# Block 2 of a two-block model on one core: recurrence without GpSimd, output product begun tile by tile, narrower waits at three stage borders

## The reference, cut to what matters

```python
q, k, v, u, y_branch, g_att, g_rec = jnp.split(z, SPLITS, axis=-1)
y_att = neighbourhood_attention(q, k, v, rpb[l]) @ w_att_o[l]
u = centred_depthwise_conv(u, conv_w[l], conv_b[l])
h_fwd = rg_lru(u, w_rg_a[l, 0], b_rg_a[l, 0], w_rg_i[l, 0], b_rg_i[l, 0], lru_lambda[l, 0], False)
h_bwd = rg_lru(u, w_rg_a[l, 1], b_rg_a[l, 1], w_rg_i[l, 1], b_rg_i[l, 1], lru_lambda[l, 1], True)
y_rec = ((h_fwd + h_bwd) * jax.nn.gelu(y_branch)) @ w_rec_o[l]
mixed = jax.nn.sigmoid(g_att) * y_att + jax.nn.sigmoid(g_rec) * y_rec
x = x + mixed @ w_out[l]
...
def rg_lru(u, w_a, b_a, w_i, b_i, lam, reverse):
    r_gate = jax.nn.sigmoid(block_diag_linear(u, w_a, b_a)).astype(jnp.float32)
    i_gate = jax.nn.sigmoid(block_diag_linear(u, w_i, b_i))
    log_a = -LRU_C * r_gate * jax.nn.softplus(-lam.astype(jnp.float32))
    a = jnp.exp(log_a)
    mult = jnp.sqrt(jnp.maximum(-jnp.expm1(2.0 * log_a), 0.0))
    bx = mult * (i_gate * u).astype(jnp.float32)
```

## Time and profile before

| | us |
|---|---|
| median of 3 runs | 2997.16 (2996.86 to 3001.26) |
| the profiled execution | 2997.03 |
| its span, first to last instruction | 2995.2 |
| TensorE busy in it | 2883.7 (96%) |
| VectorE, ScalarE, GpSimd busy | 1736.0, 1310.8, 279.7 |
| mean granted TensorE clock | 0.984 |

### The profile page before, as it was taken

The page is one execution under the profiler, slowest core; times in us unless marked ns, Lnnn a source line. Parts: engine busy times, 40 slices in busy tenths (PEclk is TensorE's granted clock), DMA queues, the critical chain, the costliest instruction groups (busy, mean ns, idle before and its releaser), DMA issues.

```text
span 2995.2 us, 34460 instructions
## 1 busy us (share of the span) xinstructions
PE 2883.7 (96%) x13080; PEld 2283.8 (76%) x13080; DVE 1736.0 (58%) x2404; ACT 1310.8 (44%) x2112; POOL 279.7 (9%) x167
## 2 busy tenths in 40 slices
PE   7999999999999999998999999998999999999997
PEld 5777777888888878886766777776787888878885
DVE  4333355235866666777455425998324866666785
ACT  4444452114655544454354314666114555554452
POOL 4122410000000000001222101222000000000000
PEclk9999999999999999999999999999999999999998
DMA  3111111113344385440312111111113343375441
GB/s 113 36 36 37 42 36 43 57 57 126 127 155 150 135 305 165 152 133 22 135 50 58 35 57 45 54 43 43 49 42 120 130 155 144 152 281 179 152 137 57
DMA packets 84971, 302.70 MB, mean 101 GB/s; under 512 B 9424, under 2 KB 9552, under 8 KB 78544
## 3 DMA queue, kind: packets, MB, share of 16 engines
q1 hardware_dynamic: 83088, 294.31, 28.7%
q10 hardware_dynamic: 1728, 6.29, 0.7%
HBM read 225.07 MB, written 75.50 MB: 100 GB/s over the span
## 4 chain that ended last, share of the span: by engine, by line
PE 56%; issue 33%; DVE 6%; ACT 3%; POOL 2%; DMA 0%; POOLq 0%; DVEq 0%; SPq 0%; ACTq 0%
PE ps L2230 16%; PE ps L371 12%; PE ps L2496 5%; PE pa L2496 5%; PE ps L2525 4%; PE pa L2525 4%; PE ps L2374 2%; PE pa L2274 2%; PE pa L2302 1%; PE ps L2541 1%; PE pa L2283 1%; DVE th L2063 1%; POOL tm L699 1%; POOL sqsum L617 1%; DVE tm L2066 1%
## 5 line engine op out<-in xcount | busy, mean ns | idle before, releaser
L361 DVE TENSOR_TENSOR w_lo<-w_raw,w_hi 128x1024 fp32r<-128x1024 f32 x134 | 181.4, 1355 | 516.8 <-ACT w_hi L355 516.7
L355 ACT ACTIVATE w_hi<-w_raw 128x1024 fp32r<-128x1024 f32 x134 | 141.3, 1055 | 450.1 <-PE ps L371 292.5
L371 PE MATMUL ps<-a_hi,w_hi 128*128 128x512 f32 x896 | 286.4, 401 | 20.8 <-DVE w_lo L361 9.4
L371 PE MATMUL ps<-a_lo,w_hi 128*128 128x512 f32 x896 | 284.2, 399 | 0.0
L371 PE MATMUL ps<-a_hi,w_lo 128*128 128x512 f32 x896 | 283.5, 398 | 0.0
L2230 PE MATMUL ps<-a_hi,w_hi 128*128 128x512 f32 x704 | 237.3, 418 | 22.7 <-DVE w_lo L361 10.1
L2230 PE MATMUL ps<-a_lo,w_hi 128*128 128x512 f32 x704 | 225.8, 402 | 0.0
L2230 PE MATMUL ps<-a_hi,w_lo 128*128 128x512 f32 x704 | 225.6, 401 | 0.0
L1149 ACT ACTIVATE krh<-k_rraw 128x512 fp32r<-128x512 f32 x192 | 121.1, 630 | 234.2 <-PE ps L2525 124.6
L371 PEld LDWEIGHTS ps<-a_hi,w_hi 128*128 128x128 f32 x896 | 170.6, 192 | 66.0 <-issue 14.8
L1845 DVE TENSOR_TENSOR krl<-k_rraw,krh 128x512 fp32r<-128x512 f32 x192 | 132.7, 691 | 136.0 <-ACT krh L1149 135.5
(11 more groups left out here) (325 smaller groups left out, 6056.3 us busy)
## 6 DMA issues: line engine op xcount, KB each, us to landing
w_raw<-wstream SPq DMA_DIRECT2D x134, 512.0 KB, 3.5
k_rraw<-hff SPq DMA_DIRECT2D x224, 256.0 KB, 2.7
hff<-hbuf SPq DMA_DIRECT2D x32, 1024.0 KB, 3.9
wA<-wff SPq DMA_DIRECT2D x16, 2048.0 KB, 7.8
hff<-hbuf SPq DMA_DIRECT2D x32, 768.0 KB, 3.3
w_raw<-wff SPq DMA_DIRECT2D x32, 512.0 KB, 4.1
f_raw<-wff SPq DMA_DIRECT2D x32, 512.0 KB, 4.5
hres<-zt SPq DMA_DIRECT2D x16, 512.0 KB, 2.6
```

The lines of the kernel that those rows point to most:

```text
L355: nc.scalar.activation(w_hi[:, slot], w_raw[:, slot], ACT.Copy).then_inc(s_whi, 1)
L361: nc.vector.tensor_tensor(w_lo[:, slot], w_raw[:, slot], w_hi[:, slot].bitcast(F32), ALU.subtract).then_inc(s_wlo, 1)
L371: mm = nc.tensor.matmul(out[0:m, c], w[0:kp, slot, wofs:wofs + m], x[0:kp, k, c * HC:(c + 1) * HC], start=first and n == 0, stop=last and ...
```

## The change

1. **GpSimd** does nothing more in `rec`. Its three operations per tile become VectorE instructions: `u_lo`, the sum of the directions at the head of `output`, and `gelu_arg`, one scalar_tensor_tensor that takes the place of both VectorE's polynomial and GpSimd's product.
2. **Guard on ScalarE**: a Relu with scale -1 (L1304 of the changed kernel) between tanh and exp of each direction; VectorE's two guard instructions go. ScalarE's gelu tanh moves behind the square roots, and the one-column tanh `warm` goes.
3. **Release by direction**: the first two gates of a tile wait for the forward scan of the tile before alone, the last two for the backward one. `(1 + i) * u` (`input_part`) is done for both directions as soon as their gates are out.
4. **Order** in a tile on VectorE: input parts, weight split, `gelu_arg`, convolution of the next tile, forward direction, weight split, `u_lo`, `gelu`, backward direction, weight split, output. On ScalarE `u_out` splits the next y unit before it reads u out. The gate unit's split covers the 512 columns that are used, not 1024.
5. **mrg2**: VectorE splits the first weight unit before any `rec_lo`; `rec_hi` of tiles other than 7 waits for scans; TensorE's first projected product waits for its `r_lo` tiles one by one.
6. **out2**: `a_hi`/`a_lo` of tiles 0 to 5 are split before the last two projected products, tiles 6 and 7 right behind their merges; the split of the unit out2+1 comes last on VectorE.
7. **Borders**: VectorE's last `a2_lo` comes before the last weight split of the attention; TensorE enters `gat0`, `rec` and `out2` with waits for the one buffer that each product overwrites, not with `enter`.

```diff
-            nc.scalar.activation(w_hi[:, slot], w_raw[:, slot], ACT.Copy).then_inc(s_whi, 1)
+            nc.scalar.activation(w_hi[:, slot, 0:n], w_raw[:, slot, 0:n], ACT.Copy).then_inc(s_whi, 1)
...
-            u_lo(0)
-            for c in range(KT):
-                pool.wait_ge(sem("s_gpoly"), c + 1)
-                nc.gpsimd.tensor_tensor(gt[:], gt[:], y_in[:, c % 2], ALU.mult).then_inc(sem("s_gin"), 1)
-                if c < KT - 1:
-                    u_lo(c + 1)
-                pool.wait_ge(sem("s_scan"), 2 * c + 2)
-                nc.gpsimd.tensor_tensor(tm[:, 0], tm[:, 0], tm[:, 1], ALU.add).then_inc(sem("s_dirs"), 1)
...
+                if c:
+                    split_hi(act, u + 2, u % 2, (u + 2) // 2, t + 1)
                 nc.scalar.activation(ur[c % 2][:, 2:2 + S], pair_flat(t), ACT.Identity, bias=V("b_in", 12 + c)
...
-                    if c and o == 0:
-                        act.wait_ge(sem("s_scan"), 2 * c)
+                    if c and o % 2 == 0:
+                        act.wait_ge(sem("s_scan"), 2 * c - 1 + o // 2)
...
+                    nc.scalar.activation(tm[:, d], tm[:, d], ACT.Relu, scale=-1.0).then_inc(sem("s_neg"), 1)
...
-                act.wait_ge(sem("s_gin"), c + 1)
-                nc.scalar.activation(gt[:], gt[:], ACT.Tanh, scale=0.7978845608028654).then_inc(s_thr, 1)
                 for d in range(2):
                     act.wait_ge(sem("s_neg"), 2 * c + d + 1)
                     nc.scalar.activation(tm[:, d], tm[:, d], ACT.Sqrt).then_inc(sem("s_root"), 1)
-
-                if c:
-                    act.wait_ge(sem("s_warm"), c)
-                nc.scalar.activation(warm[:], ones[:, 0:1], ACT.Tanh).then_inc(sem("s_warm"), 1)
+                act.wait_ge(sem("s_gin"), c + 1)
+                nc.scalar.activation(gt[:], gt[:], ACT.Tanh, scale=0.7978845608028654 * 0.044715).then_inc(s_thr, 1)
...
+            act.wait_ge(s_mm, st.t + 11)
+            for k in range(6):
+                merged_hi(2, k)
+            split_hi(act, st.u + 15, (st.u + 13) % 2, (st.u + 15) // 2, st.t + 14)
+            merged_hi(2, 6)
+            split_hi(act, st.u + 16, (st.u + 14) % 2, (st.u + 16) // 2, st.t + 15)
+            merged_hi(2, 7)
...
+                    a2_lo(npair - 1)
                     weights(3 * npair + EXTRA)
-                    a2_lo(npair - 1)
...
             for c in range(KT):
-                guards(c)
+                input_part(c, 0)
+                input_part(c, 1)
+                unit_gates(c)
+                gelu_arg(c)
+                if c < KT - 1:
+                    conv(c + 1)
                 direction(c, 0)
                 if c < KT - 1:
                     unit_y(c + 1)
+                    u_lo(c + 1)
+                gelu(c)
                 direction(c, 1)
-                gelu(c)
...
-                st = enter("out2") if b == 2 else STAGES["out1"]
+                st = STAGES[f"out{b}"]
+                if b == 2:
+                    pe.wait_ge(s_outA, st.a)
...
-            st = enter("gat0")
+            st = STAGES["gat0"]
...
-            st = enter("rec")
+            st = STAGES["rec"]
...
+                if t == st.t:
+                    pe.wait_ge(s_outA, st.a)
+                elif t == st.t + 1:
+                    pe.wait_ge(s_outD, st.d)
+                else:
```

More of the change, by code:

```diff
@@ L983, in _, with merged_hi @@
                     unit_split(U_GP + 2 * n + 3)
+            def merged_hi(b, k):
+                if b == 1:
+                    act.wait_ge(sem("s_mrg"), k + 1)
+                else:
+                    act.wait_ge(s_outD, STAGES["mrg2"].d + k + 1)
+                nc.scalar.activation(a_hi[:, k], (mres if b == 1 else res)[:, k], ACT.Copy, scale=0.5
+                                     ).then_inc(sem("s_mhi"), 1)
             def out_stage(b):
@@ L988, in out_stage @@
                 n = 1 if b == 1 else 3
[L989 to L996, removed]
+                if b == 1:
+                    act.wait_ge(s_mm, st.t - 1)
+                    for k in range(KT):
+                        merged_hi(1, k)
                 gain = "g_mlp" if b == 1 else "g_ln2"
@@ L2057, in conv, with input_part @@
                 ins.then_inc(sem("s_conv"), 1)
+            def input_part(c, d):
+                dve.wait_ge(s_outA, st.a + 3 + 6 * c + 2 * d + 2)
+                i = th[:, 2 * d + 1]
+                nc.vector.scalar_tensor_tensor(out=i, in0=i, scalar=1.0, in1=uc[:, c % 2], op0=ALU.add, op1=ALU.mult
+                                               ).then_inc(sem("s_iu"), 1)
             def direction(c, d):
@@ L2074, in direction, with gelu_arg, u_lo @@
                 ins.then_inc(sem("s_scan"), 1)
-            def guards(c):
+            def gelu_arg(c):
                 dve.wait_ge(sem("s_gsq"), c + 1)
[L2080 to L2083, removed]
+                nc.vector.scalar_tensor_tensor(out=gt[:], in0=gt[:], scalar=1.0 / 0.044715, in1=y_in[:, c % 2],
+                                               op0=ALU.add, op1=ALU.mult).then_inc(sem("s_gin"), 1)
+            def u_lo(c):
+                dve.wait_ge(sem("s_uh"), c + 1)
+                if c:
+                    dve.wait_ge(s_mm, st.t + 6 * c + 1)
+                nc.vector.tensor_tensor(ul[:], uc[:, c % 2], uh[:].bitcast(F32), ALU.subtract).then_inc(sem("s_ul"), 1)
             def gelu(c):
@@ L2144, in gated @@
                 nc.vector.tensor_tensor(r, r, zt[:, z], ALU.add).then_inc(s_outD, 1)
-            for n in range(3):
-                rec_lo(n, REC_ORDER[n])
             split_lo(dve, st.u + 2, st.u % 2, st.t + 1)
-            for n in range(3, KT):
+            for n in range(KT):
                 rec_lo(n, REC_ORDER[n])
@@ L2156, in _ @@
                         gated(t1, 2 * i + o - 2, o - 2)
-            for o in range(2):
-                split_lo(dve, st.u + 15 + o, (st.u + 13 + o) % 2, st.t + 14 + o)
-                gated(st.t + 14 + o, 6 + o, o)
+            for k in range(6):
+                merged_lo(2, k)
+            split_lo(dve, st.u + 15, (st.u + 13) % 2, st.t + 14)
+            gated(st.t + 14, 6, 0)
+            merged_lo(2, 6)
+            gated(st.t + 15, 7, 1)
+            merged_lo(2, 7)
+            split_lo(dve, st.u + 16, (st.u + 14) % 2, st.t + 15)
             out_stage(2)
@@ L2557, in _ @@
                         pe.wait_ge(s_outD, st.d + o + 1)
+                    else:
+                        pe.wait_ge(s_outA, st.a - 1 + o)
                     for k in range(4):
@@ L2604, in projected, with gate_pair @@
                 mm.then_inc(s_mm, 1)
-            with pe.Fori(0, KT // 2 - 1) as i:
+            def gate_pair(i):
                 for o in range(2):
@@ L2609, in _ @@
                     unit8(pe, st.u + 4 * i + o + 1, (st.u + o + 1) % 2, st.t + o + 1, a_hi, a_lo)
-                pe.wait_ge(sem("s_rlo"), KT)
+            gate_pair(0)
+            pe.wait_ge(s_wlo, st.u + 4)
+            for n, k in enumerate(REC_ORDER):
+                pe.wait_ge(sem("s_rlo"), n + 1)
+                mm = product((st.u + 1) % 2, pa[:, 0:2], r_hi, r_lo, k, n == 0, n == KT - 1)
+            mm.then_inc(s_mm, 1)
+            projected(st.u + 4, st.u % 2, 1, 1)
+            with pe.Fori(1, KT // 2 - 1) as i:
+                gate_pair(i)
                 for o in range(2):
```

44 lines of the change are left out of this document (18 added, 26 removed).

## The result

The changed kernel takes 2947.19 us (median of 4 runs, 2945.3 to 2949.14) beside 2997.89 us (4 runs, 2996.86 to 3001.26) for the kernel before: ratio 0.9829, 95% interval 0.9812 to 0.9846. That is 51 us less, against 56 forecast. The profiled execution took 2945.80 us, its span is 2944.0 us, 51.2 shorter than before.

What follows compares the result with a forecast made beforehand. TensorE was taken as the bound: its work fixed, only idle time and low-clock matmuls removable. Gains 5.5 + 6.7 + 30.5 + 4.7 + 8.5 = 55.9 off 2997.03 gave 2941 us; forecast case 2933 to 2948, range 2932 to 2964.

Steps and rivals of the forecast that it cites:

- Gat0: Before `gat0`, TensorE's idle 3.80 us waiting for `att_lo` and 1.7 us of clock loss go: 5.5 us.
- rec entry: Entering `rec`, TensorE's idle 3.67 us waiting for the read-out `res` and 3.0 us of clock loss go: 6.7 us.
- The cause in the loop: In the tile loop, three GpSimd operations per tile lengthen VectorE steps, costing about 6.6 us; without them TensorE sets the pace.
- The tile: Each tile of `rec` takes 28.65 us at TensorE's pace instead of 33.0; seven tiles gain 30.5 us.
- after 6.35: In a tile, the gates end after 6.35 us, with the weight split ahead of u's read-out making one start 0.8 later.
- Mrg2: In `mrg2`, the first weight split ends earlier, gaining 4.7 us; a wait of about 4.2 us and its clock loss stay.
- G+26.5: End of the first weight split in `mrg2`, 26.5 us after the last gate product ends (G), instead of G+31.2.
- Out2: Before `out2`, TensorE's idle 6.08 us behind the last merge and splits and 2.4 us of clock loss go: 8.5 us.
- A: Rival: VectorE sets the loop's pace after all, tile 30.4 us, 2953 to 2965 us; chance 0.13.
- C: Rival: the borders gain only half, since the wait behind each is as late; 2953 us, chance 0.07.
- B: Rival: VectorE pays what GpSimd gives up, tile stays 33.0 us, only borders gain 25.4; 2972 us, chance 0.06.
- D: Rival: ScalarE, not GpSimd, causes VectorE's 3.42 us steps, so the kernel gets slower, 3017 us; chance 0.04.

Runs made afterwards that it cites:

- e_borders: The kernel before with only the edits of gat0, the rec entry, mrg2 and out2, keeping its tile loop; 2979.87 us, ratio 0.9926.
- e_moves: The kernel before with GpSimd's three operations per tile done by VectorE at the same places; 2983.2 us, ratio 0.9936.
- e_ulo_pool: The changed kernel with `u_lo` alone back on GpSimd; 2951.8 us, ratio 0.9827.
- e_urfirst: The changed kernel with u read out of PSUM before the next weight split, as in the kernel before; 2947.52 us, ratio 0.9815.
- e_guard_dve: The changed kernel with the two guards back on VectorE, behind the convolution; 2950.92 us, ratio 0.9825.
- e_psum: The changed kernel with u read out first, mrg2's first weight split earlier, and each tile's second and third gates in idle PSUM banks; 2939.22 us, ratio 0.9788.

## Why the prediction was right, step by step

The time came at 2947.2 us, inside the forecast of 2933 to 2948 but near its upper end. Given the scatter of whole executions it could as well have come somewhat above it; the stages are the better test.

- **Gat0**, 5.5 forecast, 5.8 measured; **rec entry**, 6.7 for idle time and clock. In that stage 6.3 was gained, and 6.8 in e_borders, which reads u first; the 0.5 between them is the order of edit 4.
- **The cause in the loop** was right: GpSimd made VectorE's steps long (e_moves, e_ulo_pool), and once they are gone TensorE paces the tile (e_urfirst, e_guard_dve, e_psum).
- **The tile**, 28.65 forecast, 29.1 measured (203.6 / 7): the term that was mis-sized is the gate products, "after 6.35". They took 6.71 (from the split released by u at 1851.16 to the last gate at 1857.87). I counted the split ahead of the read-out, but no time for the hand-over from TensorE to ScalarE. The rows show one each time: the second gate starts at 1853.28 and is read 1.71 us later, for 1.39 us of matmuls (48 in 11.16 us, so six in 1.39). I also took the period of 28.61 of the old tile 0 as the row that carries the sum, though it has the other order on ScalarE. Seven times 0.43 is 3.0 us, most of the difference between 56 and 51.
- **Mrg2**, 4.7 forecast and G+26.5 for the split's end; measured 4.5 (31.19 against 26.65 from the last gate to TensorE's start) and G+26.5 (2058.84 - 2032.33). The clock loss behind it, which I had left out as unchanged, was 2.3 us before (0.67 over 7 us) and 1.5 after: 0.8 more gained.
- **Out2**, 8.5 forecast, 8.5 measured (19.67 against 11.16 between the last projected product and the first of `out2`).
- **The rest**: that nothing moves outside was right in kind, but the two parts differ by 1.0 and 1.3 us between the two traces, within what they do from trace to trace.
- **Rivals**: A did not come, although VectorE was busy 25 of 29 us in a tile; it was never late. C did not come: the borders alone gained 25.0 us (e_borders). B and D fell by e_moves and e_ulo_pool. The slack was there, 2.1 us by the forecast: the backward scan of tile 0 ends at 1853.79 and the third gate, which needs it, is read at 1856.38, 2.6 us later.
- **The idle times in the loop** that I named began at 2.02 us. The trace also has 1.44 and 1.71 us (1866.54, 1932.07), and behind these the clock stayed at 1.00.

## What to carry to other kernels

A GpSimd operation beside a full VectorE cost VectorE more here (2.1 to 2.2 us) than doing the work itself (1.2): look for steps of one kind with two durations before counting busy shares. When TensorE paces a loop, look for what is left over its matmuls in the read-out of PSUM, where it was here: read first, split weights afterwards, and use idle banks before shaving anything on the other engines. Stage times between marks on one engine resolve 0.2 us where whole executions scatter by ten.

## What the runs showed of the hardware

- A two-input VectorE step of 128x1024 takes 1.22 us alone and up to 3.4 with a GpSimd operation beside it (3.42 in e_ulo_pool, where GpSimd's own takes 3.02). The one-input guard took 0.69 us in e_moves and 1.69 on average in the kernel before.
- The length of one idle time did not decide whether the clock fell. Over the next 7 us it was 0.76 behind 2.02 and 2.85 us (kernel before), but 1.00 behind 2.82 us (e_guard_dve); in e_borders it was 1.00 behind 2.97 us and 0.76 behind 2.98 us:

```profile
1924.43:1931.43 7.00, 6.72 (x28) 5.21 (x29) 6.82 (x5) 5.98 (x6) 2.11 (x1) 1.00 0.25 75
1989.96:1996.96 7.00, 7.00 (x23) 5.57 (x24) 6.82 (x5) 4.69 (x5) 2.10 (x1) 0.76 0.24 75
```

  Behind idle times of 3.67 us and more it fell each time in the kernel before and in e_borders; behind 1.71 us and less, and behind stalls of 0.83 repeated every tile, it never did. What decides between 2.0 and 3.0 us is open.
- Two square roots between their table loads cost ScalarE 1.28 us per load and nothing else: the load at 1848.71 ends where the root starts, 1850.00.
- The same code ahead of and behind the changed stages took up to 8.6 and 6.3 us more in one trace than in another; what makes it is open.
